# Two DRAM buffers for blocks on their way to columns, and a new order of loads and hand-backs in the MLPs of a two-layer trunk

## The reference

```python
def squared_relu_mlp(u, w1, w2):
    hdn = jnp.square(jax.nn.relu(jnp.einsum("bsd,df->bsf", u, w1)))
    return jnp.einsum("bsf,fd->bsd", hdn, w2)
...
    for i in range(DEPTH):
        u = rmsnorm(h, norm_mix[i])
        m = conformer_conv_module(...) if i % N_MIXERS == 0 else short_gated_conv(...)
        h = h + m
        h = h + squared_relu_mlp(rmsnorm(h, norm_mlp[i]), mlp_w1[i], mlp_w2[i])
        h = h + per_layer_embedding(h, p[i], norm_ple[i], ple_w_proj[i], ple_w_gate[i])
    return rmsnorm(h, norm_final)
```

## Time and profile before

| | |
|---|---|
| median of three runs | 2291.85 us |
| the profiled execution's own time | 2290.21 us |
| its span | 2288.3 us |
| PE, DVE, ACT busy | 2225.0, 1724.7, 1244.9 us |
| granted TensorE clock, mean | 0.991 |
| moved by the DMA engines | 503.53 MB, 220 GB/s over the span |

### The profile page before, as it was taken

One profiled execution on the slowest core, in us unless ns is written; L12 is line 12 of the kernel. 1 busy time (PEld: TensorE's weight loads), 2 busy tenths in 40 slices (PEclk: granted clock), 3 DMA queues, 4 the chain that ended last, 5 costly groups with the idle time before them and its releaser, 6 DMA issues.

```text
span 2288.3 us, 29712 instructions
## 1 busy us (share of the span) xinstructions
PE 2225.0 (97%) x10152; PEld 1839.4 (80%) x10152; DVE 1724.7 (75%) x1897; ACT 1244.9 (54%) x1542; POOL 156.9 (7%) x183
## 2 busy tenths in 40 slices
PE   8999998999999999988999999999999999999988
PEld 8998787888888888866888888878888888888766
DVE  6998877788787787656766667677877877876665
ACT  5666655556555555555644444555565555564554
POOL 3887000000000000000000000000000000000000
PEclk9999999999999999999999999999999999999999
DMA  9453587767767767587777677777677677675873
GB/s 342 157 172 124 182 288 239 236 203 239 227 197 237 233 195 236 161 267 232 222 244 216 215 247 227 240 227 231 215 232 221 209 238 223 203 240 155 270 248 110
DMA packets 499526, 503.53 MB, mean 220 GB/s; under 512 B 261040, under 2 KB 299120, under 8 KB 498416
## 3 DMA queue, kind: packets, MB, share of 16 engines
q1 hardware_dynamic: 497600, 499.71, 69.9%
q10 hardware_dynamic: 1696, 1.67, 0.2%
q0 software_dynamic: 144, 1.05, 0.1%
HBM read 464.62 MB, written 37.75 MB: 220 GB/s over the span
## 4 chain that ended last, share of the span: by engine, by line
PE 70%; DMA 5%; DVE 4%; ACT 3%; issue 2%; SPq 1%; DVEq 0%; ACTq 0%
PE acc L677 12%; PE acc L679 12%; PE acc L678 12%; PE acc L654 8%; PE acc L655 8%; PE acc L656 8%; PE tp L677 3%; PE tp L679 3%; PE tp L678 3%; DVE wlo L1493 2%; DMA pT<-staged 2%; DMA pl<-in_mlp_w 1%; DMA staged<-prows 1%; DMA raw<-in_mlp_w 1%; ACT work L924 1%
## 5 line engine op out<-in xcount | busy, mean ns | idle before, releaser
L1493 DVE TENSOR_TENSOR wlo<-pl,whi 128x1024 fp32r<-128x1024 f32 x372 | 444.8, 1207 | 162.1 <-ACT whi L1009 156.2
L1009 ACT ACTIVATE whi<-pl 128x1024 fp32r<-128x1024 f32 x372 | 386.3, 1048 | 318.6 <-PE acc L679 205.2
L1323 DVE TENSOR_TENSOR wlo<-raw,whi 128x1024 fp32r<-128x1024 f32 x248 | 297.0, 1220 | 146.0 <-ACT whi L904 143.3
L904 ACT ACTIVATE whi<-raw 128x1024 fp32r<-128x1024 f32 x248 | 257.7, 1055 | 215.6 <-PE acc L656 215.2
L1009 ACT ACTIVATE whi<-raw 128x1024 fp32r<-128x1024 f32 x196 | 207.4, 1058 | 205.4 <-PE acc L679 124.9
L1493 DVE TENSOR_TENSOR wlo<-raw,whi 128x1024 fp32r<-128x1024 f32 x196 | 239.5, 1222 | 54.7 <-ACT whi L1009 51.2
L654 PE MATMUL acc<-whi,b_hi 128*128 128x512 f32 x672 | 263.2, 392 | 8.6 <-DVE b_lo L1427 7.0
L655 PE MATMUL acc<-wlo,b_hi 128*128 128x512 f32 x672 | 262.1, 390 | 0.0
L656 PE MATMUL acc<-whi,b_lo 128*128 128x512 f32 x672 | 262.0, 390 | 0.0
L677 PE MATMUL acc<-whi,a_hi 128*128 128x512 f32 x596 | 234.2, 393 | 10.5 <-DVE wlo L1493 10.5
L677 PE MATMUL acc<-whi,b_hi 128*128 128x512 f32 x596 | 233.6, 392 | 10.2 <-DVE wlo L1493 10.2
(11 more groups left out here) (218 smaller groups left out, 4051.9 us busy)
## 6 DMA issues: line engine op xcount, KB each, us to landing
pl<-in_mlp_w SPq DMA_DIRECT2D x368, 512.0 KB, 5.0
raw<-in_mlp_w SPq DMA_DIRECT2D x72, 1024.0 KB, 5.9
raw<-in_sc_w_in SPq DMA_DIRECT2D x48, 1024.0 KB, 6.5
raw<-in_cf_w_pw SPq DMA_DIRECT2D x64, 512.0 KB, 8.9
raw<-in_ple_w_gate SPq DMA_DIRECT2D x32, 1024.0 KB, 8.2
staged<-prows SPq DMA_DIRECT2D x240, 128.0 KB, 3.3
pT<-staged SPq DMA_DIRECT2D x56, 512.0 KB, 6.5
raw<-in_cf_w_pw SPq DMA_DIRECT2D x16, 1024.0 KB, 7.4
```

The source lines that it names most:

```text
L904: nc.scalar.activation(whi[:, e % SLOTS, :, :], raw[:, e // 2, 2 * (e % 2):2 * (e % 2) + 2, :], ACT.Copy).then_inc(hi_ready, 1)
L1009: nc.scalar.activation(whi[:, ring(parity, i), c, :], source[:, c, :], ACT.Copy).then_inc(slot_hi, 1)
L1323: nc.vector.tensor_tensor(wlo[:, e % SLOTS, :, :], raw[:, e // 2, 2 * (e % 2):2 * (e % 2) + 2, :], whi[:, e % SLOTS, :, :].bitcast(F32), A ...
L1493: nc.vector.tensor_tensor(wlo[:, ring(parity, i), c, :], source[:, c, :], whi[:, ring(parity, i), c, :].bitcast(F32), ALU.subtract).then_i ...
```

## The change

There are five parts.

1. A second DRAM buffer `staged_odd`. In the MLPs and for the block that `load_gate` stages, blocks with odd number use it, and `stage_early` waits no longer for the way back before it.
2. The first step's fields: field 1 goes out ahead of the way back of the first hidden block, field 2 behind it, then the four plain parts, then field 3. Before, fields 1 to 3 went out behind the plain parts.
3. `HI0` goes from 4 to 6 in `STEP`. `END` keeps 4 (`HI0_END`). `HI1_END` goes from 11 to 10.
4. In `END` the two slots cut in halves are no longer the first two ("e") but ("d", 1, 0) and ("d", 1, 1).
5. In `END` the second output block is turned at slot 18, the first is split at slot 19, and the ways back go out at slots 15 and 19 (before 17 and 21).

```diff
@@ -43,8 +43,8 @@
 STEP = (("m", 1, 0), ("e", 3, 0), ("m", 1, 1), ("e", 3, 1), ("m", 5, 0), ("e", 3, 2), ("m", 5, 1), ("e", 3, 3),
         ("d", 0, 0), ("m", 6, 0), ("d", 0, 1), ("m", 6, 1), ("d", 0, 2), ("d", 0, 3),
         ("d", 1, 0), ("m", 7, 0), ("d", 1, 1), ("m", 7, 1), ("d", 1, 2), ("d", 1, 3)) + LATE
-END = (("e", 3, 0, 0), ("e", 3, 0, 1), ("e", 3, 1, 0), ("e", 3, 1, 1), ("e", 3, 2, None), ("e", 3, 3, None),
-       ("d", 0, 0, None), ("d", 0, 1, None), ("d", 1, 0, None), ("d", 1, 1, None),
+END = (("e", 3, 0, None), ("e", 3, 1, None), ("e", 3, 2, None), ("e", 3, 3, None),
+       ("d", 0, 0, None), ("d", 0, 1, None), ("d", 1, 0, 0), ("d", 1, 0, 1), ("d", 1, 1, 0), ("d", 1, 1, 1),
        ("d", 0, 2, None), ("d", 0, 3, None), ("d", 1, 2, None), ("d", 1, 3, None),
        ("d", 2, 0, None), ("d", 2, 1, None), ("d", 2, 2, None), ("d", 2, 3, None),
        ("d", 3, 0, None), ("d", 3, 1, None), ("d", 3, 2, None), ("d", 3, 3, None))
@@ -58,8 +58,8 @@
 COMBO = {5: 0, 6: 1, 7: 2, 3: 3}
 BANK = {1: 0, 2: 0, 7: 1, 4: 1, 5: 2, 3: 2, 6: 3}
 IN_PLACE_AFTER = {5: 1, 6: 5, 7: None, 4: 6}
-OUT_ADD, OUT_TURN, OUT_SPLIT = (15, 17, 21), (15, 19), 20
-HI0, HIDDEN1, HI1, HI1_FIRST, HI1_END = 4, 3, 12, 13, 11
+OUT_ADD, OUT_TURN, OUT_SPLIT = (15, 17, 21), (15, 18), 19
+HI0, HI0_END, HIDDEN1, HI1, HI1_FIRST, HI1_END = 6, 4, 3, 12, 13, 10
 
 
 def ring(parity, i):
@@ -197,9 +197,9 @@
     POOL_TAPS = 9
     SHARE = 3 * D // 8
     Q = P // TILES
-    staged = nc.dram_tensor("staged", [P, 2 * NB], F32).ap()
+    staged, staged_odd = (nc.dram_tensor(f"staged{i}", [P, 2 * NB], F32).ap() for i in range(2))
     emb_kept = nc.dram_tensor("emb_kept", [P, DEPTH, 2, D], F32).ap()
-    staged_rows = staged.rearrange("(f j) (k n) -> f (j k) n", j=TILES, n=P)
+    staged_rows, staged_odd_rows = (b.rearrange("(f j) (k n) -> f (j k) n", j=TILES, n=P) for b in (staged, staged_odd))
 
 
 
@@ -418,13 +418,11 @@
                     if q == 0 and back is not None:
                         back()
 
-            def stage_begin(T, earlier=None):
+            def stage_begin(T, rows=staged_rows):
 
                 sp.wait_ge(tr_ready, T + 1)
-                if earlier is not None:
-                    sp.wait_ge(xt_ready, 16 * earlier + 16)
                 for i in range(TILES):
-                    nc.sync.dma_start(staged_rows[:, :, i * Q:(i + 1) * Q], turned[i * Q:(i + 1) * Q, :, :]
+                    nc.sync.dma_start(rows[:, :, i * Q:(i + 1) * Q], turned[i * Q:(i + 1) * Q, :, :]
                                       ).then_inc(staged_ready, 16)
 
             def stage(T):
@@ -434,13 +432,13 @@
 
             def stage_early(r):
 
-                stage_begin(r.T, r.x - 1)
+                stage_begin(r.T, staged_odd_rows if r.j % 2 else staged_rows)
 
             def take_back(r):
 
                 sp.wait_ge(staged_ready, 64 * r.T + 64)
                 sp.wait_ge(operand_ready, 2 * (r.o - 1) + 2)
-                nc.sync.dma_start(xt, staged).then_inc(xt_ready, 16)
+                nc.sync.dma_start(xt, staged_odd if r.j % 2 else staged).then_inc(xt_ready, 16)
 
             def exchange(r):
                 if not r.transposed:
@@ -534,13 +532,17 @@
                 for j in range(2):
                     load(up.b + j, w1, j * NB, 0, exchange(Result(before, BLOCKS - 2 + j)))
                 for f in range(4):
+                    if f == 1:
+                        stage_early(Result(up, 0))
+                    if f == 3:
+                        for n in range(4):
+                            if n == 0:
+                                sp.wait_ge(combo_ready, layer + 1)
+                            plain(layer, 0, n)
                     sp.wait_ge(lo_ready, HALVES * (up.b + 1) + 2 * f + 2)
                     field(layer, 0, f)
-                    if f == 0:
-                        exchange(Result(up, 0))()
-                        sp.wait_ge(combo_ready, layer + 1)
-                        for n in range(4):
-                            plain(layer, 0, n)
+                    if f == 1:
+                        take_back(Result(up, 0))
                 load_step(layer, 0)
                 with sp.Fori(1, STEPS - 1) as k:
                     load_step(layer, k)
@@ -567,7 +569,7 @@
                     for j in range(2):
                         if i == OUT_TURN[j] - 1:
                             stage_early(Result(down, j))
-                        if i == OUT_TURN[j] + 2:
+                        if i == OUT_TURN[j] + j:
                             take_back(Result(down, j))
                 if layer:
                     sp.wait_ge(slot_used, first_slot(layer, STEPS))
@@ -1045,7 +1047,7 @@
                         if i == HIDDEN1:
                             act.wait_ge(slot_used, base)
                             hidden(before[1], up_free)
-                        if i == HI0:
+                        if i == (HI0_END if end else HI0):
                             operand_hi(before[0].x, 2 * parity, hid)
                         if i == (HI1_END if end else HI1):
                             operand_hi(before[1].x, 2 * parity + 1, hid)
```

## The result

The changed kernel takes **2267.98 us** in the median (2267.83 to 2268.62, four runs) against 2291.49 us of the kernel before in the same comparison: ratio 0.9894, 95% interval 0.9882 to 0.9906, or 23.5 us less. Forecast were 2256 us and a range from 2238 to 2275. The sign and the range were right; a third of the forecast gain did not come.

The account below looks back on a forecast made before the run. TensorE, busy 2225.0 of 2288.3 us, was taken as the bound, so only its pauses and slow stretches could go. Terms of 4.5 + 3.1 + 2 + 3 + 5 = 17.6 us a layer, 35.2 in all, gave 2256 us, range 2238 to 2275.

Parts of the forecast that it names:

- rival 1: Closing step and gate block: DMA engines bind, so what is issued earlier lands no earlier; 2274.6 us, chance 0.16.
- First step: Field 1 lands 6 us earlier, pauses remain at slots 1 to 3; gain 4.5 us a layer, bounds 1 and 7.5.
- I take sharing: First step: transfers share the DMA engines, so the way back takes its median of 6.5 us and lands at 370.4.
- rival 2: First step: transfers end in order of issue, slots come 2 us sooner; 6.5 us a layer, 2252 us, chance 0.12.
- Middle steps: Six a layer: the pause at slot 4 goes with the later operand split; 3.1 us a layer, 6.3 in all.
- Rival 4: Steps: a way back holds SP, so plain parts behind it come too late; slower, 2323 us, chance 0.04.
- Start of the closing step: Two more parts go out while SP stood, pauses at slots 3 and 4 go; 2 us a layer, bounds 0.5 and 2.5.
- End of the closing step: First output block's way back lands at about 1015 to 1016.5; gain 3 us a layer, bounds 0 and 5.
- Gate block: First gate block: two buffers let the fourth output block's way there land earlier; 5 us a layer, bounds 2 and 9.
- ACT's wait ahead of slot 19: Sign of being right, end of the closing step: ACT's wait for the way back is below 2 us.
- PE's pause in the gate block: Sign of being right, first gate block: PE's pause is 1 to 3 us.
- PE's pauses in the first step: Sign of being right, first step: pauses of 4 to 5 us in all, the longest at slot 3.

Follow-up runs that it names:

- p1_fields: Kernel before with only the first step's new order of loads, one DRAM buffer: 2283.65 against 2291.86 us, ratio 0.9966.
- p2_hi0: Kernel before with only the first block's operand split moved from slot 4 to 6 in the six middle steps: 2284.32 us, ratio 0.9963.
- p3_two_buffers: Kernel before with the second DRAM buffer alone, no wait for the way back before a new way there: 2293.18 us, ratio 1.0000.
- b2_tiles_later: Changed kernel with the gate's third and fourth tile issued at slots 16 and 20 of the closing step instead of 12 and 18: 2269.51 us, ratio 0.9897.
- g1: Changed kernel with the 2 MB load of kept embeddings moved behind the fourth output block's way back: 2261.83 us, ratio 0.9867.
- b1: Changed kernel with gate block loads ordered way there, first tile, way back, second tile, embeddings: 2257.69 us, ratio 0.9853.
- b3: Changed kernel with b1 and b2_tiles_later together: 2255.30 us, ratio 0.9843.
- g3_one_buffer_wait: g1 with each MLP output block's way there again waiting until the way back before it has landed: 2258.80 us, ratio 0.9862.
- b4: b3 with layer 1's final norm gains loaded behind the embeddings and DVE's wait moved to their first use: 2250.37 us, ratio 0.9815.

## Why the prediction was right, and where it was not

**The total: right, nearer to a rival than to the forecast.** The measured 2267.98 us are 12 us above the forecast 2256 and 6.6 below the 2274.6 of rival 1.

**First step: the time right, its way to the landing by luck.** Forecast 9 us for both layers, measured 8.2 in the profiles and 8.2 with p1_fields alone. The landing of the way back (6.3 us after its issue, 6.5 taken) and the three pauses came as worked out from there. But the 6.5 were a median over the whole kernel, and the reason given for them was that transfers share the engines ("I take sharing"). The table under "First step" shows the order of rival 2: field 1 lands first, the way back 2.4 us behind it, and what was issued later lands later. In the whole trace of the changed kernel, 2 of SP's 940 transfers land after the one issued behind them, by at most 0.74 us. By the Trainium skill (DMA: Bandwidth & Descriptors, Queues, rings and completion order) each DMA engine consumes a queue's descriptors in ring order; these landings agree with it. Rival 2's order was right and its sizes were not: it had field 1 land some 5.3 us after its issue and the way back 1.7 behind it, together about 4 us after the way back's issue, and the trace has 6.4 and 2.4. The four DMAs of the way there, still landing until 365.2, are a likely part of it; no run shows how large.

**Middle steps: right.** Forecast 6.3 us (6.2 when summed as 3.1 a layer); 7.6 in the profiles, 7.5 with p2_hi0. The pauses also cost a tenth of a microsecond in the matmul behind each, which the forecast left out. Rival 4 (SP held by a way back in the steps) did not come: there is no new pause. The sentence that the second buffer gives nothing there holds with p3_two_buffers.

**Start of the closing step: the cause right, the size off.** Forecast 4 us, 2.6 in the profiles. The term had half a microsecond for "its way back is issued some 1.5 us later"; PE loses 1.8 us there. The lateness was right (1.4 us, counted from the start of the closing step) and the flight is as before: 8.3 us from issue to landing, after 8.0. Before, it landed at 986.1 and ACT came to the split at 988.34, a slack of 2.2 us. Now it lands 1.7 us later in the step, and ACT comes 3.3 us sooner. The forecast did not set the landing against the moment at which ACT comes.

**End of the closing step: mis-sized.** Forecast 6 us, 2.7 in the profiles. The step that failed is "issued when the "there" DMAs have landed, about 1011 ... landed at about 1015 to 1016.5". Counted from the end of the turning (1003.13 before, 994.27 now), that is an issue after 7.9 us and a landing after 11.9 to 13.4. Measured are 9.4 and 13.9 (16.7 before): SP's issue of the way there took 6.84 us instead of 5.64. A second step was left out: the split stands one slot earlier, so ACT comes to it 9.2 us after the turning and no longer 12.6. That uses up the whole 2.8 us by which the way back lands sooner; ACT waited 4.73 us instead of 4.17. b2_tiles_later shows that the queue ahead has a part: with 1 MB less there, the issue takes 4.05 us and ACT waits 1.98. Why the issue became longer than before is not shown. A cost that the prediction did not name also came: in layer 1 DVE stands 1.45 us for the final gains.

**Gate block: wrong.** Forecast 10 us, 1.7 in the profiles, nothing with p3_two_buffers. The step that failed is "With two buffers the "there" DMAs are issued at 1040 ... I take them as landed at 1047 instead of 1051.3". They were issued at once, and landed not a bit earlier, since the 2 MB of embeddings and a tile were in the queue ahead. Of the 1.7 us, 1.5 are in layer 1, whose gate block begins with PE's pause of 1.8 us for the gains; the later pause is likely shorter because of it. This was rival 1 (issued earlier, landed no earlier), true at this one place and not at the start of the closing step. The row had it: a share of 0.90 of the DMA engines. I gave the mechanism 0.16 for the whole and nothing by place; a term of 5 us a layer stood on one assumed landing. g1, b1 and b3 show that the pause itself was worth what the forecast said (11 us a layer down to 3 to 4 in b1), but the lever is what is ahead in the queue and not the buffer, whose wait g3_one_buffer_wait put back at no loss.

**The clock.** It stayed at 1.00 in the first step of layer 0 and at the end of the closing step, not in the first step of layer 1 (0.97) nor in the gate block (0.89). With b4 it stays in the gate block too.

**The signs.** Of those named for "right" two did not come: ACT's wait ahead of slot 19 is 4.73 us (below 2 forecast), and PE's pause in the gate block 5.86 (1 to 3 forecast). Both belong to the two terms that were too large. PE's pauses in the first step are 3.7 us in all, a little under the 4 to 5.

A way back of 0.5 MB takes between 3.7 us (g3_one_buffer_wait, issued at 1037.70) and 6.3 us (b1_gate_order) in the same gate block, with one tile of 1 MB ahead of it. In both it lands 1.2 to 1.4 us behind that tile, and so it does in g1_emb_behind (5.6 us). What differs is the tile: 5.8 us from its issue in g3_one_buffer_wait, 7.5 in b1_gate_order and 8.2 in g1_emb_behind.

Open: why the tile differs so much, with one profiled execution of each. And no run tried larger packets in the way there, which takes 5.6 us in 128-byte packets even with little ahead of it.

## What to carry to other kernels

When a transfer waits for a buffer, look at what its DMA queue holds at that moment before buying a second buffer: if much stands ahead in the queue, as here, the issuer only stands in the issue instead of in the wait, and the landing stays. Then order is the lever: put large loads that are used late behind small transfers that are used next, and check that they do not end up in front of the next small one. When a transfer is made to land earlier, ask also when its user comes: moving the user forward can take the gain again. When a place is mended, a wait hidden behind it (here a wait placed well ahead of its first use) is the next bound.

## What the runs showed of the hardware

Issuing four DMAs of 128 KB each took SP 2.9 us with little in the queue (b1_gate_order) and 8.7 us when some 3.5 MB had been issued in the 5.3 us before (changed kernel); no engine shows this time as busy, but the chain of waits of the changed kernel's page has "SPq L425" with 2% of the span. From the end of that issue to the way back are 2.6 us after 8.70 us of issue (changed kernel, 1038.09 to 1040.67) and 2.7 us after 2.92 us (b1_gate_order, 1033.49 to 1036.17), so in these two what stood ahead delayed the way there in its issue and not behind it.

Transfers of one queue landed in the order of their issue, all but 2 of 940 in the changed kernel. A way there in 128-byte packets filled the DMA engines (share 0.96) at 143 GB/s, where large loads moved 441 GB/s (b1_gate_order).
